# Moving the attention's value products directly in front of the next unit's transposes, in a one-core decoder layer

## The reference, cut to what matters

```python
s_c = einsum('bgrqd,bgcd->bgrqc', qb, kc)      # 31 compressed keys
p_c = masked_softmax(s_c - slopes * d_c, vis_c) * any(vis_c)
o_c = einsum('bgrqc,bgcd->bgrqd', p_c, vc)
...
p_s = masked_softmax(s_s - slopes * d_s, d_s >= 0)   # selected keys
o_s = einsum('bgrqk,bgqkd->bgrqd', p_s, v_g)
...
p_w = masked_softmax(s_w - slopes * d_w, vis_w)      # window keys
o_w = einsum('bgrqk,bgkd->bgrqd', p_w, v_w)
return gb[..., 0:1] * o_c + gb[..., 1:2] * o_s + gb[..., 2:3] * o_w
```

## Time and profile before

| | us |
|---|---|
| median of 3 runs | 1253.72 (1253.67 to 1253.89) |
| the profiled execution | 1253.25 |
| its span, first to last instruction | 1251.5 |
| TensorE busy in the span | 1231.2 (98%) |
| DVE busy | 835.3 (67%) |
| ACT busy | 630.7 (50%) |
| granted TensorE clock, mean (not a time) | 1.0 |

### The profile page before, as it was taken

One profiled execution on the slowest core, in us unless ns is written; L12 is line 12 of the kernel. 1 busy time (PEld: TensorE's weight loads), 2 busy tenths in 40 slices (PEclk: granted clock), 3 DMA queues, 4 the chain that ended last, 5 costly groups with the idle time before them and its releaser, 6 DMA issues.

```text
span 1251.5 us, 17700 instructions
## 1 busy us (share of the span) xinstructions
PE 1231.2 (98%) x6709; PEld 1052.9 (84%) x6709; DVE 835.3 (67%) x1585; ACT 630.7 (50%) x1193; POOL 88.8 (7%) x78
## 2 busy tenths in 40 slices
PE   6999999999999999999999999999999999999998
PEld 5998898889978998878978888888888888888887
DVE  4426996898869996899774633333688888884221
ACT  6616667677785767766775623333433223323110
POOL 1000001500042001400040000000000000000000
PEclk9999999999999999999999999999999999999999
DMA  8612321132212322142115733335233333334341
GB/s 241 166 35 59 85 60 43 48 105 53 75 43 63 90 60 59 36 117 60 51 43 174 234 96 98 88 101 186 59 96 98 101 101 89 97 102 135 101 127 42
DMA packets 185593, 116.34 MB, mean 93 GB/s; under 512 B 25917, under 2 KB 169637, under 8 KB 185509
## 3 DMA queue, kind: packets, MB, share of 16 engines
q1 hardware_dynamic: 181879, 108.86, 30.4%
q10 hardware_dynamic: 3630, 6.35, 1.4%
HBM read 106.80 MB, written 8.39 MB: 92 GB/s over the span
## 4 chain that ended last, share of the span: by engine, by line
PE 86%; DVE 9%; DMA 2%; ACT 2%; issue 1%; SPq 0%; ACTq 0%; DVEq 0%
PE g L603 15%; PE g L605 15%; PE g L604 15%; PE t L596 4%; PE g L644 4%; PE g L646 3%; PE g L645 3%; PE ob L793 2%; PE s L777 2%; DVE w_low L1542 2%; PE s L957 2%; PE s L958 2%; PE s L959 2%; DVE piece_a L1768 2%; PE s L875 1%; PE t L699 1%
## 5 line engine op out<-in xcount | busy, mean ns | idle before, releaser
L1026 ACT ACTIVATE w_high<-wraw 128x1024 fp32r<-128x1024 f32 x175 | 185.1, 1059 | 283.6 <-DMA wraw<-in_ffn_w_up 135.7
L1542 DVE TENSOR_TENSOR w_low<-wraw,w_high 128x1024 fp32r<-128x1024 f32 x174 | 216.6, 1248 | 127.9 <-ACT w_high L1026 125.8
L603 PE MATMUL g<-hT_hi,w_high 128*128 128x512 f32 x360 | 158.4, 440 | 1.1 <-DVE hT_lo L1548 0.5
L644 PE MATMUL g<-w_high,hT_hi 128*128 128x256 f32 x512 | 151.6, 296 | 0.2 <-DVE w_low L1542 0.2
L646 PE MATMUL g<-w_high,hT_lo 128*128 128x256 f32 x512 | 144.7, 283 | 0.0
L645 PE MATMUL g<-w_low,hT_hi 128*128 128x256 f32 x512 | 144.6, 283 | 0.0
L605 PE MATMUL g<-hT_hi,w_low 128*128 128x512 f32 x360 | 141.3, 392 | 0.0
L604 PE MATMUL g<-hT_lo,w_high 128*128 128x512 f32 x360 | 140.9, 391 | 0.0
L603 PE MATMUL g<-h2T_hi,w_high 128*128 128x512 f32 x352 | 137.3, 390 | 0.1
L604 PE MATMUL g<-h2T_lo,w_high 128*128 128x512 f32 x352 | 137.0, 389 | 0.0
L605 PE MATMUL g<-h2T_hi,w_low 128*128 128x512 f32 x352 | 137.0, 389 | 0.0
(11 more groups left out here) (347 smaller groups left out, 2517.4 us busy)
## 6 DMA issues: line engine op xcount, KB each, us to landing
wraw<-in_w_in SPq DMA_DIRECT2D x152, 256.0 KB, 3.3
wraw<-in_ffn_w_up SPq DMA_DIRECT2D x88, 256.0 KB, 3.2
wraw<-in_ffn_w_down SPq DMA_DIRECT2D x44, 256.0 KB, 3.3
wraw<-in_w_proj_b SPq DMA_DIRECT2D x32, 256.0 KB, 3.2
yT_lo<-spill SPq DMA_DIRECT2D x6, 1024.0 KB, 9.0
spill<-piece_e ACTq DMA_DIRECT2D x16, 256.0 KB, 4.1
wraw<-in_w_proj_a SPq DMA_DIRECT2D x16, 256.0 KB, 3.2
wraw<-in_w_out SPq DMA_DIRECT2D x16, 256.0 KB, 3.3
```

Source lines behind the costliest of these rows:

```text
L603: nc.tensor.matmul(gb[par][:, :], w, hi, start=k == 0, stop=False)
L644: nc.tensor.matmul(out_, hT[0][:, k, cols], w, start=k == 0, stop=False)
L1026: nc.scalar.activation(whi[slot_of(u)][:, :, :], wraw[u % 2][:, :, :], ACT.Copy).then_inc(w_hi, 1)
L1542: V.tensor_tensor(wlo[slot_of(u)][:, :, :], wraw[u % 2][:, :, :], whi[slot_of(u)][:, :, :].bitcast(F32), ALU.subtract).then_inc(w_lo, 1)
```

## The change

Three places of the tensor program are written in another order; nothing is added or left out, and no other engine's program changes.

1. In each unit n = 1 to 7, `weighted_values(n - 1)` no longer stands at position 1 but directly in front of `p_transposes((0, 1))`: at position 3, in unit 7 at position 5.
2. In the block OX, `weighted_values(7)` no longer stands at position 2 but directly in front of the first transposes of x at position 3.
3. In OC, the first half of the compressed scores no longer stands at position 1 but at position 3, directly in front of the second half.

```diff
-                block_of(u0 + OC, {1: lambda: comp_scores((0, 1)), 3: lambda: comp_scores((2, 3)), 5: lambda: scores(1),
+                block_of(u0 + OC, {3: lambda: (comp_scores((0, 1)), comp_scores((2, 3))), 5: lambda: scores(1),
                                    **late_y})
...
                     between = {at[0]: lambda: p_transposes((0, 1)), at[1]: lambda: p_transposes((2, 3))}
                     if n:
-                        between[1] = lambda: weighted_values(n - 1)
+                        between[at[0]] = lambda: (weighted_values(n - 1), p_transposes((0, 1)))
                     elif g:
                         between[0] = lambda: y_transposes(g - 1, (3,))
...
-                block_of(u0 + OX, {2: lambda: weighted_values(7), 3: lambda: xz_transposes(0), 4: lambda: xz_transposes(1),
+                block_of(u0 + OX, {3: lambda: (weighted_values(7), xz_transposes(0)), 4: lambda: xz_transposes(1),
                               5: lambda: xz_transposes(2), 7: lambda: xz_transposes(3)})
```

## The result

| | before, us | changed, us |
|---|---|---|
| median of 4 runs each | 1253.81 | 1261.27 |
| lowest and highest | 1253.67, 1254.25 | 1260.51, 1262.6 |
| profiled execution, span | 1253.25, 1251.5 | 1261.35, 1259.6 |

The changed kernel is slower: ratio 1.0063, 95% interval 1.0051 to 1.0076. Predicted were 1261.5 us, range 1257.5 to 1264.

A forecast was written before the change was run, and what follows sets the result against it. TensorE, busy for 98% of the span, was taken as the bound: what it issues plus what it waits. Terms of 1.94 us per group, four times 7.8 us, on 1253.72 us gave 1261.5 us, range 1257.5 to 1264.

The forecast's parts named there:

- The fold in units 2, 4 and 6: DVE's fold awaits ACT's copy of the moved product, delaying TensorE's last transposes: +0.23, +0.99 and +0.73 us.
- T01: Start of TensorE's transposes of j = 0 and 1 in a unit, the prediction's zero: 309.59 in unit 4.
- low parts that follow the fold faster than 2.9 us: Sign in units 2, 4 and 6 that would show the forecast wrong; its stretches were 2.98, 3.14 and 2.88 us.
- unit 5 gives its own wait back: TensorE's earlier 0.22 us wait for DVE in unit 5 goes, leaving net +0.77 us with unit 4.
- Unit 7's product: In block OX, ACT's copy starts 0.44 us later, so the third transposes of x start 0.21 us later.
- The compressed scores: First half, complete at 121.01 in group 0, is taken by DVE at 121.47 behind ACT's bias: cover 0.46 us, no cost.
- The seams: Changes between kinds of work on TensorE, 16 places at 0.10 us: taken as zero, between 1.6 us gained and lost.
- The sum: 0.23 + 0.77 + 0.73 + 0.21 = 1.94 us per group, four times 7.8 us.
- Covered folds: Rival for units 2, 4 and 6: later folds delay nothing, time stays 1253.7 us; chance 0.08.
- paying seams: Rival on TensorE: leaving the stream costs; 36 fewer visits at 0.10 us save 3.6 us, giving 1250.1; chance 0.06.
- The piling up: Rival: DVE is late again in units 3, 5 and 7, for example 0.8 us more per group, 1264.7 us; chance 0.07.

The follow-up runs named there:

- even units only: The kernel before, with only the value products of units 2, 4 and 6 moved in front of the first transposes: 1260.08 us, ratio 1.0051.
- even units back: The changed kernel, with the value products in units 2, 4 and 6 put back to position 1: 1254.81 us, ratio 1.001.
- fold last: The changed kernel, with DVE's fold of units 2, 4 and 6 behind all four low parts of its unit: 1260.17 us, ratio 1.0052.

## Why the prediction was right

**The fold in units 2, 4 and 6** was the right mechanism and nearly the right size. ACT's copy started 0.20 us behind T01 in unit 4 (0.19 forecast), and the fold 0.82 (0.88 forecast: the step from the end of the copy to the fold took 0.03 us, not the 0.10 read in the block OX, where it is 0.10 in the changed kernel too). From the fold to the end of the low parts it took 315.30 + 1.16 - 313.32 = 3.14 us, exactly as before. The terms came out as 0.19 (0.23), 0.96 less 0.20 (0.99 less 0.22), and for unit 6 3.85 - 3.16 = 0.69 (0.73). Each was forecast 0.03 or 0.04 too high: the fold came 0.05 or 0.06 earlier than forecast, and TensorE went on 0.14 or 0.15 us behind the low parts instead of 0.13. That unit 5 gives its own wait back is borne out by even units only (9.43 against 9.63).

One sign named in the prediction could decide nothing: low parts that follow the fold faster than 2.9 us were to show it wrong, while its own term for unit 6 uses 2.88, which is also what was measured.

**Unit 7's product** cost 0.23 us (0.21). **The compressed scores** cost nothing, behind ACT's bias as forecast.

**The seams** gave nothing that could be measured. The one distance that no row had shown, from a product's short last matmul to a transpose, is 322.77 - 322.65 = 0.12 us, and the seven transposes behind it take 0.71 instead of 0.68. Together that is 0.12 + 0.71 - 0.06 - 0.68 = 0.09 us too much, where the projection paid 0.10. The Trainium skill (TensorE: Matmul & The Clock Gate, "LDWEIGHTS (loading the stationary operand)") puts a load at the column count divided by 1.2 GHz, which makes an estimate of 107 ns for 128 columns. The 0.11 and 0.12 us behind the short matmul agree with it: the load of what follows would stay uncovered there, be it a projection's or a transpose's. No run varied the load, so this reading is not shown.

**The sum** took group 1 four times, 7.8 us. Three groups gave 1.84 to 1.86 and the last 1.66, which makes 7.2; the medians differ by 7.5. The prediction's "the four groups repeat one another" does not hold for the last group: its units had rows of their own that I did not use.

**The rivals.** Covered folds and paying seams are refuted by even units back and even units only: 12 moves bring nearly all of the loss, and the other 20 gain nothing. The piling up did not happen in the changed kernel (unit 3 took 9.96 us in both) but it is no fiction: fold last produced it. My reason against it, that DVE sits idle before j = 2 in each unit, holds only as long as the fold stands ahead of that idle time.

## What to carry to other kernels

Moving work on the busiest engine is free or not by what is queued behind its result elsewhere: follow the result through the next engine's program, and compare its arrival with the moment at which that engine gets to it, not with the moment at which somebody needs it. Where an engine takes work in order, put first what the bottleneck waits for; here the low parts of j = 0 and 1, put ahead of the fold and the weights' low part, were worth 7.6 us, as much as the change lost. And when an instruction is moved off the critical place, ask whether the stretch it goes to has idle time: the same fold of 0.6 us fitted in ahead of DVE's idle place, and behind it made the next unit 0.59 or 0.98 us longer.

## What was unexpected of the hardware

In unit 4 DVE's stretch from the fold to the low parts takes 3.14 us, and the same three instructions in unit 6 take 335.28 + 1.14 - 333.54 = 2.88. Their own durations differ by 0.02 us at most; in unit 4 they don't overlap (314.04 comes 0.03 behind the fold's end), in unit 6 each starts 0.07 to 0.08 ahead of the end of the one before. It is so in all four groups, before and after. It goes with the fold and not with its neighbours: in fold last, where convolutions follow the folds, the next instruction starts 0.72 us behind the start of unit 4's fold (316.90 to 317.62) and 0.60 behind that of unit 2 (295.95 to 296.55). Unit 4's fold is the only one of the three that works on partitions 64 to 127 (`DH * (r % 2)` in `out_fold`); those of units 2 and 6 work on 0 to 63. No run here varies the partitions alone.
